# Projection jobs cut into four pieces and dealt over the units of the scan by their time on TensorE

## The reference, cut to what matters

```python
px = (h_x * (1.0 + ca_x) + sa_x) @ w_in[l]
pc = (h_c * (1.0 + ca_c) + sa_c) @ w_in[l]
# columns of px, pc: qa ka va | qb kb vb | qc ic fcf fcb gc | qd kd vd
o_a = _window_attn_latent(_rope2d(qa), _rope2d(ka), va, ...)      # A: window
o_b = _global_attn_latent(_rope2d(nq(qb)), _rope2d(nk(kb)), vb, ...)  # B: nq, nk are RMS norms
o_c = _hgrn_mixer((qc, ic, fcf, fcb, gc), ...)                    # C: gated scan, both directions
o_d = _neigh_attn_latent(qd, kd, vd, ...)                         # D: neighbourhood
h_x = LN(ALPHA * h_x + ga_x * (concat(o_a, o_b, o_c, o_d) @ w_out[l]))
h_x = LN(ALPHA * h_x + gf_x * conv_ffn(h_x ...))
```

## Time and profile before

| what | us |
|---|---|
| median of 3 runs | 2172.31 (2172.22 to 2176.0) |
| the profiled execution, its own time | 2184.93 |
| its span from first to last instruction | 2183.1 |
| PE busy | 1991.6 (91%) |
| DVE busy | 1400.0 (64%) |
| POOL busy | 998.0 (46%) |
| ACT busy | 823.7 (38%) |
| mean granted TensorE clock | 0.93 |

### The profile page before, as it was taken

How to read it: one execution, slowest core, us unless ns; L and a number is a source line. 1 busy time by engine, 2 the same in 40 slices (tenths; PEclk the granted TensorE clock), 3 DMA queues, 4 the chain that set the end, 5 groups by cost and what they waited for, 6 DMA issues and landing times.

```text
span 2183.1 us, 32973 instructions
## 1 busy us (share of the span) xinstructions
PE 1991.6 (91%) x12812; PEld 1701.3 (78%) x12812; DVE 1400.0 (64%) x2711; ACT 823.7 (38%) x1584; POOL 998.0 (46%) x750
## 2 busy tenths in 40 slices
PE   6898988989998899999989998798898988999997
PEld 3678988867787788888878878697886776888786
DVE  3229988775586998999943362897877672222444
ACT  2233524346633222222243343342445633333442
POOL 1236755520154464333353334675624257655543
PEclk7998977999998889999999999887899999999999
DMA  7450100120021332333321121111030112222321
GB/s 319 174 193 21 40 21 20 40 112 2 21 78 39 116 116 100 130 118 116 116 78 68 49 97 59 39 40 39 21 131 2 40 58 77 97 97 97 116 87 68
DMA packets 26938, 177.31 MB, mean 81 GB/s; under 512 B 2720, under 2 KB 3744, under 8 KB 7712
## 3 DMA queue, kind: packets, MB, share of 16 engines
q1 hardware_dynamic: 22544, 157.90, 19.8%
q10 hardware_dynamic: 4240, 17.30, 2.0%
HBM read 171.00 MB, written 4.19 MB: 80 GB/s over the span
## 4 chain that ended last, share of the span: by engine, by line
PE 64%; DVE 16%; POOL 7%; issue 7%; ACT 3%; DMA 2%; DVEq 0%; SPq 0%; POOLq 0%; ACTq 0%
PE PS L1145 22%; PE PS L1070 17%; PE PS L830 5%; PE PS L836 4%; PE PS L1006 3%; PE PS L1031 3%; DVE W L1508 3%; PE PS L990 2%; PE PS L1126 1%; DVE W L1793 1%; DVE U L1694 1%; PE PS L921 1%; POOL WL L2087 1%; PE PS L996 1%; DVE W L1724 1%
## 5 line engine op out<-in xcount | busy, mean ns | idle before, releaser
L1145 PE MATMUL PS<-XH,WS 128*128 128x512 f32 x2016 | 551.8, 361 | 11.8 <-POOL WS L2128 10.8
L1145 PEld LDWEIGHTS PS<-XH,WS 128*128 128x128 f32 x2016 | 365.4, 192 | 69.7 <-POOL WS L2128 7.6
L1145 PE MATMUL PS<-XL,WS 128*128 128x512 f32 x1008 | 362.4, 359 | 0.0
L2128 POOL TENSOR_TENSOR WS<-WR,WS 128x1024 fp32r<-128x1024 f32 x88 | 213.9, 2434 | 321.0 <-ACT WS L1363 320.7
L1432 ACT ACTIVATE W<-PS,PR 128x768 f32<-128x768 f32 (+1 forms) x88 | 78.0, 886 | 451.3 <-PE PS L1145 389.1
L1985 DVE SCALAR_TENSOR_TENSOR W<-PS,PR,W 128x511 f32<-128x511 f32 (+1 forms) x132 | 83.0, 656 | 215.0 <-ACT W L1432 215.0
L1145 PEld LDWEIGHTS PS<-XL,WS 128*128 128x128 f32 x1008 | 194.0, 192 | 27.6
L1508 DVE SCALAR_TENSOR_TENSOR W<-WR,SC,W 128x256 f32<-128x256 f32 x336 | 201.4, 641 | 6.0
L836 PE MATMUL PS<-EU,XH 128*128 128x256 f32 x624 | 194.9, 312 | 6.9 <-issue 6.3
L2087 POOL TENSOR_TENSOR WL<-WR,EU 128x512 fp32r<-128x512 f32 x96 | 126.5, 1339 | 140.7 <-ACT EU L1205 140.6
L836 PE MATMUL PS<-WL,XH 128*128 128x256 f32 x624 | 190.4, 305 | 0.0
(11 more groups left out here) (218 smaller groups left out, 4482.7 us busy)
## 6 DMA issues: line engine op xcount, KB each, us to landing
WR<-in_weights SPq DMA_DIRECT2D x134, 1024.0 KB, 4.8
U<-in_weights SPq DMA_DIRECT2D x10, 1024.0 KB, 6.9
U<-in_bias ACTq DMA_DIRECT2D x2, 1792.0 KB, 10.2
H<-in_x SPq DMA_DIRECT2D x1, 2048.0 KB, 10.7
H<-in_x ACTq DMA_DIRECT2D x1, 2048.0 KB, 15.2
U<-in_ln_rows ACTq DMA_DIRECT2D x2, 1024.0 KB, 4.3
WR<-in_weights SPq DMA_DIRECT2D x4, 512.0 KB, 3.6
kept<-H ACTq DMA_DIRECT2D x4, 512.0 KB, 2.6
```

What stands on the lines that cost most here:

```text
L1145: mm = pe.matmul(PS[u.pos][:, lo:hi], w[:, part, k, :], src[:, k, lo:hi], start=(k == 0 and src is xh3 and part == 0), stop=(k == KT - 1 a ...
L2128: pool.tensor_tensor(ws5[:, u.c % 2, 1], half_slot(u), ws5[:, u.c % 2, 0], ALU.subtract).then_inc(w_low, 1)
```

## The change

Every job is cut into four pieces: a tok job by token tile and half of the contraction, a feat job by quarters of the contraction. Each job of the stage now has a list of four units, one for each piece. The jobs behind the forget gate are laid end to end with a time for each (5.8 us for tok, 5.45 us for latent feat, 2.9 us for context feat), that length is divided evenly over 25 units, and each piece goes to the unit in which it begins. The last piece of a job carries what followed the job before: the signal, and the turn of the job two before it. The waits stand before the first piece. The job's slot in the tables of the other engines (`j.at`) is the unit of its last piece.

By these tables the last pieces fall as follows. Layer 0: QA in units 3, 4, 5 as before; KVA in 7, 8, 9, QB in 10, 11, 12, KVB in 13, 14, 15, each one unit later than before; VD in 16, 17, 18 (15 to 17 before); QD in 19, 20, 21, 21 (18 to 21 before); KD in 22, 23, 24, 24 (22, 23, 24, 24 before). Layer 1: QA 4, 5; KVA 6, 8, 9 (6, 7, 8 before); QB 10, 11 (9, 11); KVB 12, 14, 15 (12, 13, 14); VD 16, 17, 18 (15, 16, 18); QD 20, 21 (19, 20); KD 22, 23, 24, 24 (21, 22, 23, 24); FCB 0, 1, 2, 3 (0, 0, 1, 2).

The weights of the next slot are listed one unit after the slot before it begins. They are listed two and two, or all four in one unit where the slot begins within less than three units (QD in layer 0; KVA, KVB, QD and KD in layer 1). The order of the slots is the same in both layers. A buffer for modulation weights moves from column 17920 to 3072 of `U`, and the code gains a branch for an order in which FCF is not fourth, which neither layer uses.

```diff
+    span = lambda p: 5.8 if p[0] == "tok" else 2.9 if p[2] else 5.45
+    total = sum(span(p) for _, p in flow)
+    jobs, at = [], 0.0
+    for i, (key, part) in enumerate(early):
+        jobs.append((key, part, [i - 2] * PIECES))
+    for key, part in flow:
+        steps = [at + span(part) * q / PIECES for q in range(PIECES)]
+        jobs.append((key, part, [int(t / total * UNITS) + 1 for t in steps] if gate != 3
+                     else [int(t / total * (UNITS + 1)) for t in steps]))
+        at += span(part)
...
-        begin = first[at - 1] + (ORDER[at] == QD)
+        b, need = begin[at - 1], begin[at]
         for q in range(PIECES):
-            late.setdefault(begin + q // 2, []).append((at, q))
+            i = b + 2 if order[at] == QD else b + 1 + (q // 2 if need >= b + 3 else 0)
+            late.setdefault(i, []).append((at, q))
...
+            def project(l, j, piece):
+
+                if piece == 0:
                     if j.freed:
                         pe.wait_ge(job_act, j.freed)
                     pe.wait_ge(in_low, pieces_to(l, j.order, PIECES - 1))
...
+                if j.kind == "tok":
+                    i, ks = piece // 2, range(4 * (piece % 2), 4 * (piece % 2) + 4)
+                else:
+                    i, ks = 0, range(2 * piece, 2 * piece + 2)
+                for k in ks:
+                    for n, (wl, xl) in enumerate(((False, False), (True, False), (False, True))):
+                        mm = job_product(j, i, k, wl, xl, start=(k == 0 and n == 0), stop=(k == KT - 1 and n == 2))
+                if piece < PIECES - 1:
+                    return
+                mm.then_inc(job_sum, 1)
...
+                for q in j.turns:
+                    pe.wait_ge(roped, q.r + 1)
+                    if q.r >= 1:
+                        pe.wait_ge(qk_in, q.r)
...
-                    projections(l, beside[l, i])
+                    for j, q in pieces_at[l, i]:
+                        project(l, j, q)
```

More of the change, by code:

```diff
@@ L44, in slot_parts @@
     return [("tok", p, 0) for p in range(2 + ctx)]
-ORDER = (QC, GC, IC, FCF, FCB, QA, KVA, QB, KVB, VD, QD, KD)
+ORDERS = ((QC, GC, IC, FCF, FCB, QA, KVA, QB, KVB, VD, QD, KD),
+          (QC, GC, IC, FCF, FCB, QA, KVA, QB, KVB, VD, QD, KD))
 PIECES = 4
+UNITS = 4 * NT
 def mixer_jobs(l):
     whole = lambda s: [(("in", l, s, 0), p) for p in slot_parts(l, s)]
-    gate = whole(FCF)
-    own = whole(QC) + whole(GC) + whole(IC)
+    order = ORDERS[l]
+    gate = order.index(FCF)
+    own = [p for s in order[:gate] for p in whole(s)]
+    forget = whole(FCF)
     extra = [(("mod", 0, i, 0), ("mod", i, 0)) for i in range(MOD_FIRST, 24)] if l == 0 else []
@@ L59, in mixer_jobs @@
         mixed += [part] + extra[k * len(extra) // n:(k + 1) * len(extra) // n]
[L60 to L69, removed]
-def weight_splits(l):
[L74 to L78, removed]
+    if gate == 3:
+        mixed += forget[:2]
+        early, flow = forget[2:], [p for s in order[gate + 1:] for p in whole(s)]
+    else:
+        mixed += forget + whole(FCB)
+        early, flow = [], [p for s in order[gate + 2:] for p in whole(s)]
@@ L79, in weight_splits @@
+    return mixed, jobs
+def weight_splits(l):
+    own, jobs = mixer_jobs(l)
+    order = ORDERS[l]
+    begin = {}
+    for key, _, at in jobs:
+        begin.setdefault(order.index(key[2]), at[0])
     behind, late = {}, {}
     starts = [n for n, (key, _) in enumerate(own) if key[0] == "in"]
-    for at in range(4):
-        opening = [n for n in starts if own[n][0][2] == ORDER[at]][0] + (at == 0)
+    own_slots = sorted({order.index(own[n][0][2]) for n in starts})
+    for at in own_slots:
+        opening = [n for n in starts if own[n][0][2] == order[at]][0] + (at == 0)
@@ L104, in uses @@
             if n in behind:
[L105 to L108, removed]
+                u.append(("in", l, ORDERS[l][behind[n]], 0))
+        for i in range(-2, UNITS + 1):
+            u += [("in", l, ORDERS[l][at], 0) for at, _ in late.get(i, [])]
+            u += [key for key, _, at in beside if i in at]
         u += [("out", l, n, g) for n in range(2) for g in range(KT // KDN)]
@@ L436, in hybrid_backbone @@
             own, late = mixer_jobs(l)
-            for when, (key, part) in [(None, p) for p in own] + [(i, p) for i in sorted(late) for p in late[i]]:
+            for key, part, units_at in [(key, part, None) for key, part in own] + late:
                 j = Job()
-                j.l, j.slot, j.key, j.at = l, key[2], key, when
+                j.l, j.slot, j.key, j.units_at = l, key[2], key, units_at
+                j.at = units_at[-1] if units_at else None
                 j.kind, j.a, j.b = part
@@ L659, in hybrid_backbone @@
             if j.kind != "mod":
-                j.order = ORDER.index(j.slot)
+                j.order = ORDERS[j.l].index(j.slot)
                 first_job.setdefault((j.l, j.order), j)
@@ L890, in projections @@
[L890 to L901, removed]
-                            for i in range(2):
-                                mm = pe.transpose(tb[:, i * P:(i + 1) * P], r3[:, i, 0:P], ident)
-                        mm.then_inc(rot_tp, 1)
+                if j.kind == "tok":
+                    i, ks = piece // 2, range(4 * (piece % 2), 4 * (piece % 2) + 4)
+                else:
+                    i, ks = 0, range(2 * piece, 2 * piece + 2)
```

54 lines of the change are left out of this document (33 added, 21 removed).

## The result

The changed kernel took 2181.61 us (median of 11 runs, 2175.75 to 2187.13), the kernel before beside it 2173.65 (11 runs, 2172.03 to 2184.02). The ratio is 1.0034, 95% interval 1.0019 to 1.0049: slower by about 7.4 us by the ratio (8.0 by the medians), more than the 0.2% that a run can tell, and the time is 0.6 us above the top of the range. The forecast was 2.9 us faster.

The account below looks back on a forecast made before the run. VectorE sets the pace through the rotations, TensorE in each layer's tail. Layer 0 +1.7 and layer 1 -4.6 sum to -2.9 us, so 2169.4 us from a median of 2172.3; 8-in-10 range 2160 to 2181.

Parts of the forecast that it names:

- Layer 0, rotations one pass later: Layer 0: VectorE gets a pass 7 without rotation, +5.8 us, up to 8.7 beside GpSimd.
- Layer 0, turns in the middle of a unit: Units 8 to 10: pieces behind late turns delay VectorE's scaled queries by 1.5, 1.7 and 0.9 us, +4.1 us.
- Rival 2: Layer 0, units 8 to 11: waits before turns drop TensorE to half clock, +12 us there; 2181 us, chance 0.20.
- Layer 0, the tail: After layer 0's last turn: 64.5 us instead of 72.0, with no half clock in unit 22.
- Layer 1, VectorE's waits: Layer 1 before the tail: four VectorE waits, 10.5 us, go; unit 9 costs +1.7; sum -8.8 us.
- Layer 1, the tail: Layer 1 from unit 18: same work, but a possible wait costs +2.2 us of the 6.8 gained on entering.
- Rival 3: Units 18 (layer 0) and 21 (layer 1): late bursts of four weight pieces, +6 us on the forecast, 2176, chance 0.08.
- The weights: Low pieces one unit later: 2.6 us wait in layer 0's unit 6 covered; KD in layer 1 about 1 us.
- The sum by that rule, +2.3 us: If ports are held exclusively, layer 1's KVA and KVB bundles add 5.2 us: net +2.3 instead of -2.9.

Follow-up runs that it names:

- the kernels with one layer each: Changed kernel with one layer's jobs and weight pieces in the old units: only layer 1 in pieces 0.9984, only layer 0 in pieces 1.0035, against the kernel before.
- The kernel with the turns moved: Changed kernel, but turns due within a unit are issued behind that unit's last piece: ratio 1.0038 to the kernel before.
- the old list of weights: Changed kernel, but weight pieces listed by the rule of before, two and two, never four in one unit: ratio 0.9985 to the kernel before.
- that one line of order: ScalarE takes the jobs of unit i-1 before the exponentials of unit i+2: 0.9893 on the changed kernel, 0.9907 on the kernel before, both against the latter.

## Why the prediction was wrong

The sum was +1.7 for layer 0 and -4.6 for layer 1. The stages over the profiles say +7.0 and -1.2, the ratios of the kernels with one layer each +7.6 and -3.5. Two steps failed: the turns and jobs in the middle of a unit in layer 0, and the tail of layer 1.

**Layer 0, rotations one pass later: right.** VectorE's pass 7 has no rotation and took 248.40 - 242.61 = 5.8 us, as priced.

**Layer 0, turns in the middle of a unit: the first step that failed; the mechanism was right, its size not.** The three waits before the scaled queries are the ones named, in passes 9, 10 and 11. They are 3.0, 2.0 and 2.0 us, 7.0 together, where 4.1 was forecast. The chain from the end of VectorE's subtractions to the next scaled queries, priced at 12.1 us, took 267.60 - 253.53 = 14.1 us into pass 9 and 12.4 and 12.1 us into the next two. The first one was missed by the clock: TensorE idled 3.61 us, went on at full clock for under 1 us and then at half, so that the three pieces behind the turn took 5.8 us (granted clock 0.71) instead of 4.35. Rival 2 had this mechanism and put it into all three units; it came in one. For the other two, VectorE's own way was 1.5 and 1.4 us shorter than I had put it, so that more of the chain showed. The last turn stood 383.7 - 149.2 = 234.5 us after VectorE's start, before 375.3 - 153.2 = 222.1: +12.4 against +9.2.

**Layer 0, the tail: the right number, for half the reason.** 64.7 us against 64.5, and no half clock in unit 22. But unit 18 lasted 11.0 us and unit 21 12.6, with TensorE waiting 1.7 and 2.7 us for the bank (at 394.51 and 421.18). What the tail would be without these waits isn't shown. Layer 0 was to cost 1.7 us; this profile shows 5.2 and the mean over the profiles 7.0 (300.0 against 293.0).

**Layer 1, VectorE's waits: the gain came, by other waits than those named.** Unit 18 began 183.7 us after VectorE's start (1546.5 - 1362.8), before 192.5: -8.8 us, forecast -6.8. The waits of the earlier trace rows are gone one by one, but the unit with two pieces behind its turn, unit 9, made the next scaled queries wait 4.63 us, where +1.7 was allowed: its turn waited 4.17 us for the copy of the turn before (1463.82), and the granted clock behind it was 0.64. Up to unit 18, 3.1 us of VectorE's waits for job copies stayed, of 5.7.

**Layer 1, the tail: the second step that failed.** It was to lose 2.2 us of the 6.8; it took 65.6 us against 59.2 and gave back 6.3. The prediction had KD's bundle there, at "about 1 us". It costs much more, because it does not delay the weights' user but VectorE, and through it ScalarE's copies. Rival 3 had the place, unit 21, and the half clock behind it, but took the weights to be what TensorE waits for. Layer 1 net: -2.5 in this profile, -1.2 over three profiles of each dealing (249.2 against 250.4), against -4.6.

**The weights: half right.** The SBUF page of the Trainium skill (§ SBUF: two separate sides) says that the pair of ports is held exclusively for a whole instruction. The runs agree: each of the four subtractions that were held ended 0.15 us after the GpSimd piece beside it. The sum by that rule, +2.3 us, had the right sign, but for the wrong place. It took 5.2 us from the bundles of KVA and KVB, and splitting them gave 1.0 us before unit 18. It was not carried on to ScalarE and TensorE in the tail, where the split gave 3.8.

**What was missing altogether** is the wait of a job's first piece for its bank. Its line stood in the diff, and the prediction said of it nothing, because a whole job at the end of a unit seldom meets it: 9.5 us in both layers before, 29.3 after. The kernel with the turns moved shows that the wait keeps the whole price when no turn stands before the pieces. The PSUM page of the Trainium skill (§ Engine vs sequencer instructions) says that ScalarE's queue is strictly first in, first out; the rows agree, the copy of a finished job stood 2.98 us behind exponentials (253.57 to 256.55).

**What stays open:** 4 us of what the old list of weights gives back, or rather of the changed kernel's 7.4. The scatter between single profiles has its place (the start, and the stretch between the stages with its two lengths some 6 us apart), but not its reason; how many runs of each kernel had the longer one isn't known, and the medians may hold some of it. A third bank for the jobs would separate the bank's wait from ScalarE's order; it wasn't tried, since the scan uses all eight banks.

## What to carry to other kernels

Before cutting a job into pieces, list every wait that its first and last piece carry, and in which pass of which queue the releasing copy is made; a wait that is free at the end of a unit can be due in its middle. A copy that frees a buffer belongs in front of work that itself waits for another engine: here that one line of order was worth 20 to 31 us, and no dealing of the jobs and weights gained more than 5 over the kernel before. A burst on GpSimd is priced also by who is locked out and who waits for that engine, not only by when its own result is wanted.

## What was unexpected of the hardware

VectorE's five subtractions of two SBUF operands took 1.10 us alone, 3.06 beside two low-weight pieces and 5.23 beside four. Taken one by one (ns: least, median, longest), the row of 5.23 us is:
```profile
L1754 DVE TENSOR_TENSOR W<-W x5: 278/1355/1367, 1576.7 to 1581.7; 128x128 f32<-128x128 f32 x5
```
Four of them last about as long as a piece of GpSimd (1.31 to 1.39 us), and each ends 0.15 us after the piece beside it; the fifth takes 0.28 us. Beside two pieces it was two of the five (1.18 and 1.35 us), and the other three took 0.28. So in these rows VectorE gets exactly one such instruction done for each piece, and the burst costs by the number of its pieces as long as VectorE has as many of these instructions to run.

In the two stages of the changed kernel each of the twelve longest idle times of TensorE (3.45 to 10.54 us) was followed by a mean granted clock of 0.50 to 0.72 over the next 5 us. Behind shorter ones it was now low, now full. Windows of the changed kernel, behind idle times of 3.61, 4.17, 4.51, 1.11, 1.28 and 2.87 us (columns as in the earlier trace rows, the clock the third from the end):
```profile
258.60:264.40 5.80, 5.80 (x38) 5.67 (x37) 5.73 (x14) 0.62 (x2) 3.44 (x3) 0.71 0.00 0
1463.80:1468.50 4.70, 4.68 (x26) 4.56 (x26) 3.21 (x9) 1.60 (x7) 2.66 (x3) 0.64 0.01 3
1585.50:1590.60 5.10, 5.03 (x12) 3.77 (x12) 0.89 (x3) 0.50 (x2) 2.40 (x2) 0.54 0.00 0
383.70:387.00 3.30, 3.30 (x44) 3.10 (x42) 3.27 (x4) 1.85 (x4) 3.30 (x3) 1.00 0.02 5
217.55:222.55 5.00, 5.00 (x29) 5.00 (x30) 4.96 (x7) 0.22 (x1) 3.94 (x3) 0.66 0.02 3
1533.97:1538.97 5.00, 5.00 (x57) 4.76 (x57) 3.35 (x16) 0.04 (x1) 3.57 (x7) 1.00 0.02 5
```
